# Making the next stage's input tiles inside the previous stage, in a two-layer encoder on one core

## What is computed

```python
for i in range(DEPTH):                      # DEPTH = 2
    hn = rmsnorm(x, norm_mix[i])
    mix = mixer_ab(hn, ...) if i % 2 == 0 else mixer_c(hn, ...)
    x = x + mix
    hn = rmsnorm(x, norm_mlp[i])
    x = x + square(relu(hn @ mlp_w1[i])) @ mlp_w2[i]
return rmsnorm(x, norm_final)
```

## Time and profile before

| | us |
|---|---|
| median of 3 runs | 2340.75 |
| lowest and highest | 2329.11, 2341.82 |
| the profiled execution, whole | 2338.89 |
| its span, first to last instruction | 2337.1 |

### The profile page before, as it was taken

The page is one execution under the profiler, slowest core; times in us unless marked ns, Lnnn a source line. Parts: engine busy times, 40 slices in busy tenths (PEclk is TensorE's granted clock), DMA queues, the critical chain, the costliest instruction groups (busy, mean ns, idle before and its releaser), DMA issues.

```text
span 2337.1 us, 41439 instructions
## 1 busy us (share of the span) xinstructions
PE 2234.7 (96%) x14291; PEld 1975.8 (85%) x14291; DVE 1580.2 (68%) x2569; ACT 1050.2 (45%) x1497; POOL 166.4 (7%) x154
## 2 busy tenths in 40 slices
PE   6997769999999999999999999999999999999997
PEld 6997668888888888888888888888888888888886
DVE  7799466676567566556677777757766755755764
ACT  7642256444444444443445454445444444444442
POOL 1000000400000000000230000032000000000022
PEclk9999879999999999999999999999999999999998
DMA  8545544656656666656656656565666566566653
GB/s 227 171 132 133 123 141 135 189 171 188 197 180 195 197 184 192 197 180 184 207 159 198 182 178 189 171 189 163 194 192 188 185 198 188 184 196 187 191 185 112
DMA packets 438953, 418.02 MB, mean 179 GB/s; under 512 B 49628, under 2 KB 434860, under 8 KB 438349
## 3 DMA queue, kind: packets, MB, share of 16 engines
q1 hardware_dynamic: 435952, 414.30, 59.2%
q10 hardware_dynamic: 2908, 2.51, 0.4%
HBM read 406.35 MB, written 10.39 MB: 178 GB/s over the span
## 4 chain that ended last, share of the span: by engine, by line
PE 87%; DVE 9%; ACT 1%; DMA 1%; issue 1%; SPq 0%; ACTq 0%; DVEq 0%
PE psum L1492 53%; PE psum L1493 27%; PE psum L1489 3%; DVE ysum L884 3%; DVE whl L884 2%; PE psum L1668 1%; DVE wv L884 1%; DVE fa L884 1%; PE psum L1650 1%; DMA raw<-in_mlp_w 0%; PE psum L1645 0%; ACT whl L534 0%; DVE act L887 0%; DMA xin<-in_x 0%; PE psum L1585 0%
## 5 line engine op out<-in xcount | busy, mean ns | idle before, releaser
L884 DVE TENSOR_TENSOR whl<-raw,whl 128x1024 fp32r<-128x1024 f32 x744 | 914.9, 1240 | 523.9 <-ACT whl L534 521.5
L534 ACT ACTIVATE whl<-raw 128x1024 fp32r<-128x1024 f32 x744 | 788.5, 1061 | 844.0 <-PE psum L1493 689.2
L1492 PE MATMUL psum<-act,whl 128*128 128x512 f32 x2688 | 949.1, 397 | 11.2 <-DVE act L887 11.2
L1493 PE MATMUL psum<-act,whl 128*128 128x256 f32 x2688 | 755.2, 281 | 0.0
L1492 PE MATMUL psum<-hid,whl 128*128 128x512 f32 x2048 | 717.3, 395 | 0.7 <-DVE whl L884 0.7
L1492 PEld LDWEIGHTS psum<-act,whl 128*128 128x128 f32 x2688 | 506.2, 188 | 131.3 <-issue 12.0
L1493 PE MATMUL psum<-hid,whl 128*128 128x256 f32 x2048 | 574.3, 280 | 0.0
L1493 PEld LDWEIGHTS psum<-act,whl 128*128 128x128 f32 x2688 | 509.8, 190 | 0.1
L1492 PEld LDWEIGHTS psum<-hid,whl 128*128 128x128 f32 x2048 | 383.9, 187 | 91.1 <-DVE whl L884 1.1
L1493 PEld LDWEIGHTS psum<-hid,whl 128*128 128x128 f32 x2048 | 387.0, 189 | 0.0
L545 ACT ACTIVATE half<-psum 128x256 f32<-128x256 f32 x344 | 113.5, 382 | 295.9 <-PE psum L1493 295.1
(11 more groups left out here) (193 smaller groups left out, 1555.0 us busy)
## 6 DMA issues: line engine op xcount, KB each, us to landing
raw<-in_mlp_w SPq DMA_DIRECT2D x512, 512.0 KB, 3.9
raw<-in_c_w_qkv SPq DMA_DIRECT2D x96, 512.0 KB, 4.5
raw<-in_ab_w_in SPq DMA_DIRECT2D x64, 512.0 KB, 4.1
raw<-in_ab_w_out SPq DMA_DIRECT2D x32, 512.0 KB, 4.0
raw<-in_c_w_out SPq DMA_DIRECT2D x32, 512.0 KB, 4.4
raw<-in_s_w_glu SPq DMA_DIRECT2D x8, 512.0 KB, 3.6
bias_c<-rpb_pad SPq DMA_DIRECT2D x64, 64.0 KB, 2.6
rpb_pad<-rpbw SPq DMA_DIRECT2D x4, 889.0 KB, 10.6
```

The source lines that it names most:

```text
L534: nc.scalar.activation(whl[:, s, :, 0, :], raw[:, s], ACT.Copy).then_inc(hi_done, 1)
L884: return nc.vector.tensor_tensor(dst, s0, s1, op)
L1492: pe.matmul(bank, *big, start=first, stop=False, skip_group_check=True)
L1493: last = pe.matmul(bank[:, 0:T], *little, start=False, stop=final, skip_group_check=True)
```

## The change

There are four edits.

1. `input_high` and `input_low` take a list of tiles. A new function `residual_blocks` replaces the loops of the last 8 blocks ahead of each hand-over (OUT0, the last W2 run of MLP0, OUT1). In its block b, from b = 1, the tiles 2b-2 and 2b-1 of the next stage's input are made between the sub 1 and sub 2 preparations of the following block. Tiles 14 and 15 are made in the next stage, behind its first sub 3 preparation. ACT's and DVE's loops are written out there; PE's are not.
2. OUT0 still reads the gate's outputs while `act` is being rewritten, so these get a buffer `o_b` of their own.
3. `norm(n)` on PE moves from behind sub 1 to behind sub 2 of the first block, and `rms` and `inverse_rms` move behind the three preparations of the second block.
4. SP's load of `rpbw` moves from the start of MLP0's second run of blocks to the start of MLP0; the wait for it stays where it was.

The diff, without the lines around the changed ones:

```diff
@@ -169,6 +169,7 @@
+        o_b = at("o_b", [P, NT, 2, T], U0 + 64 * KB, F32R)
@@ -370,8 +371,6 @@
-                    sp.wait_ge(rpb_zero, 1)
-                    sp.dma_start(rpbw[:, :, 48:48 + RPB_COLS], ins["c_rpb"][0, :, 4:11, :]).then_inc(rpb_in, 16)
@@ -437,6 +436,9 @@
+                if j0 == J_MLP0:
+                    sp.wait_ge(rpb_zero, 1)
+                    sp.dma_start(rpbw[:, :, 48:48 + RPB_COLS], ins["c_rpb"][0, :, 4:11, :]).then_inc(rpb_in, 16)
@@ -550,9 +552,20 @@
-            def input_high(n, gains):
-
-                for kt in range(KT):
+            def residual_blocks(j0, n, gains, first=0):
+                for b in range(first, 8):
+                    high(0, j0 + b, 0, 3)
+                    for s in range(3):
+                        high(0, j0 + b + 1, 0, s)
+                        if b and s == 1:
+                            input_high(n, gains, (2 * b - 2, 2 * b - 1))
+                    take_halves(0, j0 + b, 0)
+            def input_high(n, gains, tiles):
+                for kt in tiles:
@@ -565,17 +578,21 @@
-            def mlp(n, j0, gains, last=False):
-                input_high(n, gains)
+            def mlp(n, j0, gains, next_gains=None):
...
-                rms(n)
+                input_high(n, gains, (KT - 2, KT - 1))
...
+                rms(n)
...
-                for k in range(1, 8):
-                    loop_blocks(j0 + 8 * k, 8, last=(last and k == 7))
+                for k in range(1, 7):
+                    loop_blocks(j0 + 8 * k, 8)
+                if next_gains is None:
+                    loop_blocks(j0 + 8 * 7, 8, last=True)
+                else:
+                    residual_blocks(j0 + 8 * 7, n + 1, next_gains)
@@ -807,7 +824,7 @@
-                nc.scalar.activation(act[:, NT + f, 0, :].rearrange("p (i j) -> p j i", j=LC),
+                nc.scalar.activation(o_b[:, f, 0, :].rearrange("p (i j) -> p j i", j=LC),
@@ -818,10 +835,8 @@
-            block_step(0, J_OUT0, 1)
-            loop_blocks(J_OUT0, 8, first=True)
-            mlp(1, J_MLP0, 32)
-            input_high(2, 16)
+            residual_blocks(J_OUT0, 1, 32, first=1)
+            mlp(1, J_MLP0, 32, next_gains=16)
@@ -838,7 +853,7 @@
-                        rms(2)
+                        input_high(2, 16, (KT - 2, KT - 1))
@@ -849,6 +864,8 @@
+                    if first and jb == 0:
+                        rms(2)
@@ -863,9 +880,8 @@
-            block_step(0, J_OUT1, 1)
-            loop_blocks(J_OUT1, 8, first=True)
-            mlp(3, J_MLP1, 48, last=True)
+            residual_blocks(J_OUT1, 3, 48, first=1)
+            mlp(3, J_MLP1, 48)
@@ -1041,11 +1057,23 @@
-            def input_low(n, gains):
-                for kt in range(KT):
+            def input_low(n, gains, tiles):
+                for kt in tiles:
...
+            def residual_blocks(j0, x0, n, gains, first=0):
+                evac = residual(x0)
+                for b in range(first, 8):
+                    i, jb = b // 2, b % 2
+                    low(i, j0, jb, 3)
+                    for s in range(3):
+                        low(i, j0, jb + 1, s)
+                        if b and s == 1:
+                            input_low(n, gains, (2 * b - 2, 2 * b - 1))
+                    evac(i, j0, jb)
@@ -1315,19 +1343,18 @@
-                now = [act[:, NT + f, k, :].rearrange("p (i j) -> p j i", j=LC) for k in range(2)]
+                now = [o_b[:, f, k, :].rearrange("p (i j) -> p j i", j=LC) for k in range(2)]
...
-            loop_blocks(J_OUT0, 8, residual(16))
-
-            def mlp(n, j0, gains, x0, h0, last=False):
-                input_low(n, gains)
+            residual_blocks(J_OUT0, 16, 1, 32)
+            def mlp(n, j0, gains, x0, h0, next_gains=None):
...
-                v.wait_ge(x_ready, x0)
...
-                inverse_rms(n)
+                input_low(n, gains, (KT - 2, KT - 1))
...
+                inverse_rms(n)
@@ -1336,10 +1363,14 @@
-                    loop_blocks(j0 + 16 * qu + 8, 8, residual(x0 + 16 * qu), last=(last and qu == 3))
-
-            mlp(1, J_MLP0, 32, 32, 0)
-            input_low(2, 16)
+                    if qu < 3:
+                        loop_blocks(j0 + 16 * qu + 8, 8, residual(x0 + 16 * qu))
+                    elif next_gains is None:
+                        loop_blocks(j0 + 16 * qu + 8, 8, residual(x0 + 16 * qu), last=True)
+                    else:
+                        residual_blocks(j0 + 16 * qu + 8, x0 + 16 * qu, n + 1, next_gains)
+            mlp(1, J_MLP0, 32, 32, 0, next_gains=16)
@@ -1380,7 +1411,7 @@
-                        inverse_rms(2)
+                        input_low(2, 16, (KT - 2, KT - 1))
@@ -1392,6 +1423,8 @@
+                    if first and jb == 0:
+                        inverse_rms(2)
@@ -1407,11 +1440,8 @@
-            block_step(0, J_OUT1, 1, evac_out1)
-            with v.Fori(1, 4) as i:
-                block_step(i, J_OUT1, 0, evac_out1)
-                block_step(i, J_OUT1, 1, evac_out1)
-            mlp(3, J_MLP1, 48, 112, 64, last=True)
+            residual_blocks(J_OUT1, 96, 3, 48, first=1)
+            mlp(3, J_MLP1, 48, 112, 64)
@@ -1510,7 +1540,7 @@
-                return o_s[:, kt] if kt < HA else act[:, kt]
+                return o_s[:, kt] if kt < HA else o_b[:, kt - HA]
@@ -1772,7 +1802,7 @@
-                    if s == 1:
+                    if s == 2:
@@ -1810,7 +1840,7 @@
-                        if first and jb == 0 and s == 1:
+                        if first and jb == 0 and s == 2:
```

## The result

The changed kernel takes 2309.71 us (median of 4 runs, 2307.66 to 2310.13) against 2335.53 us of the kernel before (4 runs); the ratio is 0.9876, with a 95% interval of 0.9852 to 0.9899. It is 1.2% faster. The four of the kernel before lie in two groups, 2329.11 and 2330.31, 2340.75 and 2341.82, and the median falls between them. The time lies under my range (2318 to 2340) and fits one of the rivals, both MLPs narrow, which I gave 0.12 and 2309.9 us.

What follows compares the result with a forecast made beforehand. PE's matmul stream was taken to bound the kernel. Hand-overs 16.5 us plus rpbw 0.74 us, all else 0, gave 17.2 us off 2340.75: 2323.5 us, with one MLP wide; 8-in-10 range 2318 to 2340.

Steps and rivals of the forecast that it cites:

- both MLPs narrow: Rival: matmul pairs in MLP0 and MLP1 both at the shorter spacing, 13.6 us under the forecast, 2309.9 us; chance 0.12.
- What bounds the kernel: PE's matmul stream from 385 us on: its waits, three hand-over gaps of 3.72 us with half clock behind, and pair spacing.
- Hand-overs: At the three stage borders: gaps go (11.16 us), lower clock behind them (5.12), slow first matmuls (0.2); gain 16.5 us.
- each gap's clock: Behind each hand-over gap PE runs 3.41 us at granted clock 0.50, losing half the work, 1.71 us.
- Moved work: In 21 blocks ahead of the hand-overs: ACT's and DVE's added input steps fit in their idle time, cost 0.
- Norm one sub later: In each MLP's first block: PE would hardly wait in either place, and DVE's later copy keeps 2 us; cost 0.
- rpbw: At 571 us in MLP0: loading the small table early removes PE's wait, gain 0.74 us, bounds 0 and 0.74.
- The spacing: Matmul pairs in a whole stage are wide (0.3531 us) or narrow (0.3464); 13.6 us for an MLP.
- The norm matmul turns the spacing over, twice in two: At each MLP's norm: narrow pairs ahead become wide behind in MLP0, wide become narrow in MLP1.
- a wide MLP0: MLP0's pairs stay at the longer spacing behind its norm; held at about 0.75.
- the one wide MLP of the forecast: Forecast case: one MLP wide and one narrow, as in the kernel before, 2323.5 us; chance 0.46.
- gap formula: The skill's N / 2.4 + 2.5 ns between warm matmuls: one spacing, 0.325 us a pair; by it 2323.5 us stands alone.

Runs made afterwards that it cites:

- e4: Kernel before with only the small `rpbw` table loaded at the start of MLP0: median 2326.04 us, ratio 0.9954 to the kernel before.
- e1: Changed kernel with norm matmul, root and reciprocal back in their old order: five executions at 2309.1 to 2312.3 us, three at 2323.5 to 2325.8, one at 2338.3.
- e9: Changed kernel with the norm back behind sub 1 and one added float32 matmul behind the first 8 blocks of each MLP: four executions at 2310.6 to 2312.5 us.
- e6: Changed kernel with the small table's load back in front of its wait: four executions at 2309.0 to 2309.6 us, six at 2321.2 to 2323.8.
- e5: The changed kernel run again, unchanged, for its spread: 2307.87 to 2309.89 us.
- e8: Changed kernel with one added float32 matmul behind OUT1's second block: median 2309.75 us, 2307.34 to 2311.38.
- p1: Changed kernel with probes at 7 inner borders of each MLP, a float32 matmul in MLP0, a wait of PE in MLP1: 2367.02 us.
- p2: Changed kernel with probes at 7 inner borders of each MLP, one float32r matmul in MLP0, four transposes in MLP1: 2326.82 us.
- e7: Kernel before, all waits kept, with one float32 matmul added to each MLP, in MLP0 a block behind the 571 us wait: median 2328.26 us, ratio 0.9958.
- e3: Changed kernel with PE waiting for all 16 input tiles at each hand-over: six executions at 2329.2 to 2332.5 us, four at 2343.4 to 2345.5.
- e2: Kernel before with only the norm moved behind sub 2, root and reciprocal behind the three preparations: nine of ten executions at 2336.9 to 2342.0 us, ratio 0.9994.

## Why the prediction was wrong, step by step

**What bounds the kernel** was right: the three gaps, their cause, the clock behind them and the wait at 571 us are all that went from PE's idle time.

**Hand-overs, 16.5 us:** right. From e4 (gaps, both MLPs narrow, 2326.04) to the changed kernel (2309.71) it is 16.3 us, where the spacing of the MLPs is the same on either side. That 1.71 us of it stands for each gap's clock is a middle value: single gaps gave from 0 to 3.1 us (last section).

**Moved work, 0:** right; OUT0's block is as long as before. The Trainium skill (SBUF — State Buffer, section Who interferes with whom) has such a pair contend with POOL. The trace agrees at the heads of the three new stages, where DVE's pair took 1.71 us instead of 0.88; but the longest single subtraction took 0.97 us, so none waited for a whole POOL sum of 1.60 us, and nothing waited for the pair.

**Norm one sub later, 0:** the term failed. I said that PE "would hardly wait in either place" and gave the move no worth. It waits 0.2 us in the old place (e1, e9). That alone is nothing, but four of nine executions of e1 then have one or two wide MLPs, and none of eight of the changed kernel. That the place does matter, in this way, is what the term had at nothing.

**rpbw, 0.74 us with bounds of 0 and 0.74:** the step that failed most. It is worth 13.2 us in the typical execution (e4), and taking it from the changed kernel costs 12 to 14 us in six executions of ten (e6). I had the row of the wait and wrote that the stage behind MLP0's norm is wide "on either side of the wait at 571 us", and so gave the wait no part in the spacing. It was a case in which it left things as they were.

**The spacing:** seen, with the right size (13.6 us; the groups lie 12 to 14 us apart), but its cause was wrong. "The norm matmul turns the spacing over, twice in two" was read from two cases that each had a gap and 3.4 us at half clock just ahead. In the changed kernel MLP0's norm has narrow ahead and narrow behind, MLP1's has wide ahead and narrow behind. With no wait at it and no gap in the same block, such a matmul is followed by narrow in all 24 cases of the traces: twelve norms of the MLPs (the changed kernel, e5, e6, e8, p1, p2) and twelve added matmuls (p1, e7, e8, e9). Behind a gap in the same block it is followed by wide in two of ten, MLP0 of before and of e3. From that wrong rule came 0.75 for a wide MLP0 and 0.12 for the case that happened; the one wide MLP of the forecast, 13.6 us, is the term that puts 2323.5 above the measured 2309.71. The Trainium skill's gap formula (TensorE: Matmul & The Clock Gate, section Back-to-back issue gap), which the page gives for an isolated matmul, has one spacing and left 2323.5 alone; the runs have two.

**What the runs show in its place:** behind a wait of PE, from 0.2 to 5.4 us, the pairs are narrow or wide, and for the same kernel the times fall in groups one MLP apart; a spacing lasts until PE waits again or meets another kind of matmul. The changed kernel has no wait of PE between 381 us and the final norm except 0.3 us in OUT1, and OUT1's spacing ends at MLP1's norm. Both its long stages are narrow in the two profiled executions, and by their times in all eight.

**Open:** why there are two spacings, and why certain waits favour one (by their times, behind the wait at 571 us wide in nine of ten in e2, in six of ten in e6). In the profiled execution of before, MLP0 was wide from its norm on, ahead of the wait at 571 us; e3 changed at the same place. Whether the gap ahead did this to the norm matmul, I have not tested; e4 has the same gap and norm and was narrow in ten of ten. What of this is due to the earlier load of the table, I have not separated.

## What to carry to other kernels

Count the matmuls per microsecond of every long stage, at full granted clock, before pricing a wait: here "PE busy 100%" covered two rates 2% apart. A short wait on the engine that bounds the kernel can cost far more than its length if it stands ahead of a long stage without another: here about 1 us of waiting came with 12 to 14 us in six executions of ten (e6). When a kernel's times fall in groups, look for the rate of a stage that differs between them, and take the waits away ahead of it first.

## What the runs showed of the hardware that I had not expected

The same stream of float32r pairs (512 and 256 columns, each with its weight load) ran at 0.3467 or 0.3533 us a pair at granted clock 1.00, unchanged over more than 2000 pairs. Four transposes between two blocks made it wide (p2), a float32 matmul of 256 columns made it narrow (e7, e8), one of float32r left it narrow (p2).

The half clock behind a wait was of different lengths. Behind the 15 waits of 3.7 us (before, e2, e4, e7, p1), PE ran 3.0 to 3.4 us at 0.50 in nine cases, 5.1 to 6.2 us in five and not at all in one, the first gap of e4. Behind the seven of 5.2 to 5.4 us (e3, p1) it ran 2.9 to 6.2 us. Waits up to 1.34 us (the row of e7) were followed by none. The rows are all engines behind the second gap of e2 (to 1207.55 us) and behind the first of e4 (to 478.96 us), which was as long:

```profile
1207.60:1213.20 5.60, 5.60 (x17) 4.76 (x18) 5.60 (x13) 4.42 (x11) 1.08 (x2) 0.50 0.12 46
...
479.00:482.40 3.40, 3.40 (x19) 2.81 (x20) 3.40 (x8) 3.40 (x10) 1.08 (x2) 1.00 0.01 2
```

So my 1.71 us for a gap's clock is the most frequent value; the lowest is 0 and the highest 3.1.
